# Products of constants in TensorE's waits, in a two-layer decoder step with a mixture of experts

## The reference

```python
def hier_moe(h, w_group, b_group, w_router, b_router, w_gate, w_up, w_down):
    ...
    g_w, g_idx = lax.top_k(g_prob, 1)
    ...
    e_w, e_idx = lax.top_k(e_prob, TOP_K_IN_GROUP)
    e_w = e_w / jnp.sum(e_w, axis=-1, keepdims=True) * g_w
    expert = g_idx * EXPERTS_PER_GROUP + e_idx
    ...
    a = jnp.einsum('nd,edf->nef', x, w_gate)
    b = jnp.einsum('nd,edf->nef', x, w_up)
    hid = jax.nn.silu(a) * b * gates[:, :, None].astype(x.dtype)
    y = jnp.einsum('nef,efd->nd', hid, w_down)
```

## Time and profile before

| | |
|---|---|
| time, median of 3 runs (lowest to highest) | 736.59 us (735.3 to 736.6) |
| profiled execution | 739.81 us |
| its span in the trace | 738.1 us |
| mean granted clock of TensorE | 0.911 |
| TensorE busy | 618.3 us (84%) |
| VectorE, ScalarE, GpSimd busy | 288.2, 128.8, 126.8 us |
| DMA | 184.81 MB, mean 250 GB/s |

### The profile page before, as it was taken

How to read it: one execution, slowest core, us unless ns; L and a number is a source line. 1 busy time by engine, 2 the same in 40 slices (tenths; PEclk the granted TensorE clock), 3 DMA queues, 4 the chain that set the end, 5 groups by cost and what they waited for, 6 DMA issues and landing times.

```text
span 738.1 us, 11033 instructions
## 1 busy us (share of the span) xinstructions
PE 618.3 (84%) x4015; PEld 416.9 (56%) x4015; DVE 288.2 (39%) x837; ACT 128.8 (17%) x284; POOL 126.8 (17%) x178
## 2 busy tenths in 40 slices
PE   5899999856999987489999997985986799998730
PEld 3677877634565543357667674574755555554410
DVE  2321230274433422435766775430136434333224
ACT  2102010220111112101112553311114011111100
POOL 0000000002233222004222321320000222331212
PEclk9999999986999999579999998998998799999865
DMA  9975003173899992898333863799736489999523
GB/s 337 292 305 227 2 26 153 71 277 126 337 410 410 410 409 86 296 387 307 114 88 95 278 230 118 240 368 398 307 143 219 173 329 411 413 410 399 219 84 109
DMA packets 60283, 184.81 MB, mean 250 GB/s; under 512 B 11676, under 2 KB 12238, under 8 KB 56006
## 3 DMA queue, kind: packets, MB, share of 16 engines
q1 hardware_dynamic: 49030, 155.52, 56.2%
q0 software_dynamic: 11200, 28.60, 10.7%
HBM read 178.96 MB, written 13.50 MB: 261 GB/s over the span
## 4 chain that ended last, share of the span: by engine, by line
PE 67%; DMA 17%; DVE 8%; SPq 3%; ACT 2%; issue 2%; POOL 0%; POOLq 0%; DVEq 0%; ACTq 0%
PE PS L1193 27%; PE PS L1270 12%; DMA hT<-in_moe_w_up 6%; PE PS L1292 6%; PE PS L1437 3%; SPq L367 3%; PE PS L1184 3%; DMA half_b<-in_b_w_o 2%; DMA zT<-y_rows 2%; PE PS L1259 2%; DMA zT<-h_rows,where 2%; PE PS L1454 2%; DMA h_rows<-tokbuf 1%; PE PS L1209 1%; PE PS L1281 1%
## 5 line engine op out<-in xcount | busy, mean ns | idle before, releaser
L1193 PE MATMUL PS<-hT,half_b 128*128 128x288 f32 x384 | 104.2, 429 | 9.6 <-DMA half_b<-in_b_w_o 6.3
L1193 PEld LDWEIGHTS PS<-hT,half_b 128*128 128x128 f32 x384 | 76.1, 201 | 33.7 <-issue 11.1
L1193 PE MATMUL PS<-hT,half_a 128*128 128x288 f32 x256 | 67.0, 419 | 3.1 <-DVE hT L799 3.1
L1270 PE MATMUL PS<-ew_in,zT 128*64 128x256 f32 x480 | 61.8, 416 | 4.1 <-DVE zT L931 2.2
L539 POOL DMA_INDIRECT y_rows<-zT,where x33 | 33.5, 1015 | 160.2 <-ACT zT L674 155.1
L1193 PEld LDWEIGHTS PS<-hT,half_a 128*128 128x128 f32 x256 | 48.7, 194 | 20.9 <-issue 4.1
L942 DVE COPY zT<-PS 128x128 f32<-128x128 f32 x33 | 9.6, 292 | 118.7 <-PE PS L1281 99.9
L1270 PEld LDWEIGHTS PS<-ew_in,zT 128*64 128x64 f32 x480 | 39.4, 151 | 29.2 <-issue 17.1
L534 POOL DMA_INDIRECT zT<-h_rows,where x35 | 36.0, 1030 | 57.3 <-DVE where L911 27.5
L901 DVE TENSOR_SCALAR zT<-lanes,slots 128x128 bf16<-128x128 bf16 (+1 forms) x222 | 39.0, 249 | 1.8 <-DVE slots L964 1.3
L545 POOL DMA_DIRECT2D h_rows<-tokbuf x2 | 1.7, 832 | 217.5 <-ACT tokbuf L657 217.5
(11 more groups left out here) (276 smaller groups left out, 917.9 us busy)
## 6 DMA issues: line engine op xcount, KB each, us to landing
ew_in<-in_moe_w_gate SPq DMA_DIRECT2D x15, 1024.0 KB
ew_in<-in_moe_w_up SPq DMA_DIRECT2D x15, 1024.0 KB
ew_down<-in_moe_w_down SPq DMA_DIRECT2D x15, 1024.0 KB
half_b<-in_moe_w_gate SPq DMA_DIRECT2D x6, 1024.0 KB
half_b<-in_moe_w_up SPq DMA_DIRECT2D x6, 1024.0 KB
half_b<-in_moe_w_down SPq DMA_DIRECT2D x6, 1024.0 KB
half_a<-in_moe_w_gate SPq DMA_DIRECT2D x6, 1024.0 KB
half_a<-in_moe_w_up SPq DMA_DIRECT2D x6, 1024.0 KB
```

Source lines behind the costliest of these rows:

```text
L1193: mm = pe.matmul(PS[:, bank, 0:T], w[:, k, col:col + P], src[:, k, :], start=(k == 0), stop=(k == KT - 1))
L1270: mm = pe.matmul(PS[f * SLOT:(f + 1) * SLOT, 2 + u, 0:EF], x_slotsT[:, u, k % 4, k // 4, :], w_in[f][:, k, :], start=(k == 0), stop=(k == ...
```

## The change

One helper is added to TensorE's list, and called in five places. `idle_products(n)` issues n products of `ident` with the first 288 columns of the constants into PSUM bank 4. Nobody reads them, they wait for nothing and signal nothing. No other engine's list changes.

```diff
         @block.tensor
         def _(pe):
+            def idle_products(count):
+
+                for _ in range(count):
+                    pe.matmul(PS[:, 4, 0:T], ident, cst[:, 0:T], start=True, stop=True)
+
...
                 mm.then_inc(S["counted"], 1)
+                if l == 0:
+                    idle_products(5)
...
                 for q in range(3):
                     table_of(q)
+                    idle_products((2, 2, 4)[q])
                 rows_up(0, gathered(0)[1], 0)
...
             experts(0)
+            idle_products(16)
             for c, (at, n) in enumerate(tok):
                 pe.wait_ge(S["yt"], c + 1)
```

## The result

| | before | after |
|---|---|---|
| median of 12 runs each, taken on one chip | 736.65 us (732.41 to 739.15) | 729.10 us (725.12 to 734.26) |
| ratio | | 0.9917, 95% interval 0.989 to 0.9944 |
| profiled execution, its span | 739.81, 738.1 us | 725.12, 723.4 us |
| mean granted clock in it | 0.911 | 0.952 |

A forecast was written before the change was run, and what follows sets the result against it. TensorE was taken to bound most of the span (67% of the chain), its waits lowering the clock. Terms 3.3 + 1.7 + 0 = 5.0 us bring the median of 736.59 to 731.6, range 729.5 to 732.8 (chance 0.43), outer bounds 725.5 to 736.

The forecast's parts named there:

- Price of a product: On TensorE, each added product is two instructions: 0.49 us at full clock, 0.98 at half.
- Layer 0's routing: 13 products in TensorE's waits bring faster row transposes and a first gate_up of 3.67 instead of 6.55: 3.3 us won.
- TensorE then does half of the time what it did none of, and I take it that the clock stays: Layer 0's routing: with products in the waits, the clock, up at 164.5 to 167, holds through the first gate_up.
- handed on through the full DMA queue: Layer 0's experts: the first waiting down load is issued 3.3 us earlier, so the saturated stretch begins and ends 3.3 earlier.
- Layer 1's routing: 8 products between tables and before the first expert: 1.7 us expected, between about -0.3 and 2.3.
- products that meet half clock between the tables: Layer 1's routing: if the clock falls there, the last four products take 3.9 us, and the net is about -0.3.
- Results: Layer 0's results, 16 products: taken as 0 us, with the clock falling again in the waits behind them.
- two waits as a coin's toss each: Layer 0's results: the clock survives a single wait of some 3 us about half the time; both must go well.
- The rival in which the clock holds: Layer 0's results: clock kept through the waits, 4.0 to 6.7 us more won, total 725 to 727.5; chance 0.27.
- The slower rival: All places: unit-matrix products with mostly zero constants don't raise the clock and run at half; +9.7 us, 746.3; chance 0.08.
- price list: The slower case's costs by place: layer 0's routing +3.0 us, layer 1 +3.2, results +3.5.
- Sum: Whole kernel: 3.3 + 1.7 + 0 = 5.0 us won, from a median of 736.59 to 731.6.

The follow-up runs named there:

- e4: Changed kernel without the sixteen products in the results, both routings keeping theirs; against the kernel before: 731.88 us, ratio 0.9963.
- e7: Changed kernel with layer 0's result waits filled further (20 products, six between the tiles' transposes, six behind the mean products); against the kernel before: 728.74 us, ratio 0.9872.
- e11: The changed kernel measured once more, on the chip of the last four kernels; against the kernel before: 729.77 us, ratio 0.9942.
- e12: The kernel of e7 measured again, beside the changed kernel; against the kernel before: 727.33 us, ratio 0.9887.
- e1: Products only in layer 0's routing (5, 2, 2, 4); against the kernel before: 735.27 us, ratio 0.9983.
- e8: e7 plus 5 products before layer 1's counts, 11 before the attention's output weights, 4 before each layer's last written-out expert; against the kernel before: 732.72 us, ratio 0.9947.
- e9: Changed kernel with 32 products in layer 0's results instead of 16; against the kernel before: 731.36 us, ratio 0.994.
- e10: e8 without the four products before the last expert, and 5 instead of 11 before the output weights; against the kernel before: 725.04 us, ratio 0.9861.
- e2: Products only at layer 1's tables (2, 2, 4); against the kernel before: 732.19 us, ratio 0.9934.
- e3: Only the sixteen products in layer 0's results; against the kernel before: 736.88 us, ratio 0.9988.
- e5: Changed kernel with each product replaced by four transposes of a constant tile; against the kernel before: 735.67 us, ratio 0.9972.
- e6: Changed kernel with each 288-column product replaced by two of 16 columns; against the kernel before: 737.89 us, ratio 1.0018.

## Why the prediction was right

- **Price of a product**, 0.49 and 0.98 us: measured 7.93 / 16 = 0.50 at full clock. Right.
- **Layer 0's routing**, 3.3 us: the profile of after shows 3.2 (182.61 to 179.42). But the step "TensorE then does half of the time what it did none of, and I take it that the clock stays" holds in only five of the nine kernels with these products (after, e4, e7, e11, e12), one profile each. In e1, e8, e9 and e10 it fell around the wait for the gathered rows and the copy, and `gate_up` took 5.3 us. The wait left before the rows' transposes was 0.81 to 1.37 us in these four and 0 to 0.80 in the five; this is no sure sign, since in layer 1 e10 kept the clock behind 0.99. The term is 3.3 where it is paid and about 1.4 where it is not; 3.3 was its upper bound, and the mean is near 2.4. Even that is measured against a `gate_up` of 6.55 us. Without products it took 6.52 in e2 and 5.01 in e3, so the kernel before doesn't always pay the whole price either, and against the mean of the three the gain is nearer to 1.9. No kernel here fills the last wait further, so what a fifth product there would do isn't tested. That the gain is handed on through the full DMA queue was right: 3.1 us are still there at the wait for weights.
- **Layer 1's routing**, 1.7 us: too low. The first `gate_up` took 3.67 us in all nine kernels whose tables had wide products; 15.58 - 13.16 = 2.4 us in the profile of after; my upper bound was 2.3. I had hedged for products that meet half clock between the tables. That was seen once, in e8, and there the same stretch took 15.43 us (560.27 to 575.70): nothing won, as I had worked it out for that case.
- **Results**, 0 us: right for the mean products. In all three kernels with just the sixteen (after, e3, e11) they took 6.66 to 6.77 us, and alone the sixteen gave 0.9988. I had two waits as a coin's toss each; the clock survived the first in all three and the second in none. The rival in which the clock holds did not come. What I can't exclude: the attention began at full clock in all three, and in one of four without them (e2; not in before and e4, and in e1 for a part). That would be up to 2.8 us where it happens. Against it, the attention was at half in e5, whose transposes stand in the same place (10.74 us), and for a part in e9, with 32 products (9.69). It is a small count and not shown.
- **The slower rival** (the constants don't raise the clock) is refuted: the clock rose at 166 under them. With thin products its price list came true in small: `gate_up` 1.45 us late, where it had 3.0. Its +3.2 for layer 1 comes to about 3.5 by the prices of the rows; nothing hangs on it.
- **Sum**: 5.0 forecast; 6.1 to 7.5 and 4.3 to 6.1 measured, by the ratios and the medians of two measurements. The parts by the profiles give 2.4 + 2.4 + 0 to 2.8 = 4.8 to 7.6. That the sum came out near has some luck in it: layer 0's term was too high in the mean, layer 1's too low. The difference of the two profiles, 14.7 us, is not all the change's. Beyond layer 0's 3.2 and layer 1's 2.4, it holds 1.7 us because the clock survived a wait of 2.40 us (269.14) that was 2.29 before and brought it down then, 1.4 on the last expert's `down`, 2.8 at the attention's start. The first of these is chance: e11 is the same program, and there the clock fell in the same wait, of 2.44 us. Of the last 3.2, about 2.2 lie behind layer 1's wait for weights, where after has no products: from there to the end it is 61.3 us before and 59.0 after, and 59.3 to 64.6 in the other profiles that have this wait. The rest lies in the results (0.5) and the attention.

## What to carry to other kernels

In this kernel a wait of 2 to 3 us in TensorE can cost twice: once as idle time, and again as up to 3 us of half-clock work behind it. Whether it does varies: at layer 0's wait for weights the clock fell in four of the seven profiles where the wait was 2.3 to 2.5 us, and in none of the six where it was 1.8 to 2.0. Products of 288 columns in the wait buy the second part back, if they end before the wait does at *half* clock too. Count them at 0.98 us each and not at 0.49 where the clock may be down, since all real work stands behind them (eleven that began at half clock in a wait of 4 to 6 us won nothing; five that began at full kept it there). Fill every wait of a chain, or expect little: the sixteen in the results paid for nothing that could be measured until the short waits behind them were filled too.

## What the hardware showed that was not expected

- **The runs scatter with the granted clock.** Over 87 executions of the kernel before, times from 729.5 to 742.2 us and mean clocks from 0.907 to 0.929 correlate at -0.88; a straight line through them gives 5.8 us less for each 0.01 more. The same program finds the clock up or down after the same wait in different executions (after and e11, above). Their standard deviation is 3.0 us, so by my estimate a change of 2 to 3 us needs dozens of runs, or the stage's own durations in several profiles. Here each kernel has one profile, and the counts over kernels stand in for that.
- **What brought the clock up.** Twelve us of mostly 16-column products, 11.85 of them busy, left it at half (e6); under the wide products and the transposes in the same places it was up after 3.4 us (e1) to 5 us (after, e5).
